# Merging the table, modulation and input-projection stages of a hybrid SSM kernel into one stage

## The reference

```python
mod = cond @ ada_w[i] + ada_b[i]
sh1, sc1, g1, sh2, sc2, g2 = jnp.split(mod, 6, axis=-1)
hn = modulate(rmsnorm(x, norm1_g[i]), sh1, sc1)       # h * (1 + scale) + shift
u = (h @ w_in).astype(f32)                            # input projection, 1024 x 1024
ab_re = mag * jnp.cos(li * dt); ab_im = mag * jnp.sin(li * dt)
# cf = (ab - 1) / lambda; bb = cf * b; then a scan over time with ab, bb, c and d
```

## Time and profile before

| What | Value |
| --- | --- |
| Median of three runs | 6785.2 us |
| Profiled execution | 6783.3 us, span 6781.7 us |
| TensorE busy | 91% of the span |
| VectorE busy | 49% |
| ScalarE busy | 31% |
| GpSimd busy | 26% |
| `ssm_tables` | 2.5 to 82.5 us |
| `ssm_input` | 83.6 to about 523 us |
| `ssm_scan` starts | 523.5 us |

### The profile page before, as it was taken

The page is one execution under the profiler, slowest core; times in us unless marked ns, Lnnn a source line. Parts: engine busy times, 40 slices in busy tenths (PEclk is TensorE's granted clock), DMA queues, the critical chain, the costliest instruction groups (busy, mean ns, idle before and its releaser), DMA issues. The chain is left out here.

```text
span 6781.7 us, 88283 instructions
## 1 busy us (share of the span) xinstructions
PE 6199.4 (91%) x29593; PEld 5085.4 (75%) x29594; DVE 3318.2 (49%) x4653; ACT 2084.9 (31%) x3429; POOL 1734.9 (26%) x1497
## 2 busy tenths in 40 slices
PE   5997888999969999999989999998996899999993
PEld 3875666888847888888868888886774788888883
DVE  5547773443364555565534322223446554556554
ACT  1215553222213433343335200001111333444434
POOL 2763223882022222222210000000001222323222
PEclk8998999999989999999989999998997999999997
DMA  4442335442225766676645534443342565677766
GB/s 140 142 126 89 107 98 174 148 141 99 86 82 187 212 188 193 201 217 200 204 107 206 207 140 158 147 155 125 127 133 99 168 192 166 202 213 243 211 205 242
DMA packets 530877, 1098.31 MB, mean 162 GB/s; under 512 B 49214, under 2 KB 127118, under 8 KB 530778
## 3 DMA queue, kind: packets, MB, share of 16 engines
q1 hardware_dynamic: 418816, 806.11, 34.4%
q0 software_dynamic: 78000, 274.13, 15.8%
q10 hardware_dynamic: 33964, 16.83, 0.8%
HBM read 835.18 MB, written 261.78 MB: 162 GB/s over the span
## 5 line engine op out<-in xcount | busy, mean ns | idle before, releaser
L127 PE MATMUL conv_p<-conv_x_lo,conv_w_hi 128*128 128x512 f32 x1536 | 601.4, 392 | 0.0
L128 PE MATMUL conv_p<-conv_x_hi,conv_w_lo 128*128 128x512 f32 x1536 | 598.7, 390 | 0.0
L129 PE MATMUL conv_p<-conv_x_hi,conv_w_hi 128*128 128x512 f32 x1536 | 598.6, 390 | 0.0
L1835 DVE SCALAR_TENSOR_TENSOR m_o<-m_pO,m_weight_of,m_gate 128x512 f32<-128x512 f32 x320 | 237.6, 747 | 723.9 <-PE m_pO L1555 383.2
L1802 DVE TENSOR_TENSOR m_w_lo<-m_w_raw,m_w_hi 128x1024 fp32r<-128x1024 f32 x496 | 577.9, 1215 | 0.0
L1610 ACT ACTIVATE m_xT_hi<-m_pX 128x512 fp32r<-128x512 f32 x320 | 191.5, 599 | 1151.8 <-PE m_pB L129 993.9
L127 PE MATMUL m_pA<-m_w_lo,m_xT_hi 128*128 128x512 f32 x1280 | 517.2, 404 | 5.7 <-DVE m_xT_lo L1813 5.7
L1551 PE MATMUL m_pO<-m_w_lo,m_hT_hi 128*128 128x512 f32 x1280 | 512.8, 401 | 0.5 <-ACT m_hT_hi L1615 0.5
L1598 ACT ACTIVATE m_w_hi<-m_w_raw 128x1024 fp32r<-128x1024 f32 x512 | 505.3, 1053 | 0.0
L129 PE MATMUL m_pA<-m_w_hi,m_xT_hi 128*128 128x512 f32 x1280 | 502.9, 393 | 0.0
L128 PE MATMUL m_pA<-m_w_hi,m_xT_lo 128*128 128x512 f32 x1280 | 500.1, 391 | 0.0
(11 more groups left out here) (388 smaller groups left out, 12641.4 us busy)
## 6 DMA issues: line engine op xcount, KB each, us to landing
m_w_raw<-in_moe_w_dram SPq DMA_DIRECT2D x384, 1024.0 KB, 7.0
conv_x_hi<-hT_hi SPq DMA_DIRECT2D x24, 2048.0 KB, 8.6
conv_x_lo<-hT_lo SPq DMA_DIRECT2D x24, 2048.0 KB, 13.3
glu_ada<-in_ada_w_dram POOLq DMA_DIRECT2D x96, 256.0 KB, 3.2
a_x<-in_x_dram SPq DMA_DIRECT2D x32, 512.0 KB, 3.6
a_ada<-in_ada_w_dram POOLq DMA_DIRECT2D x64, 256.0 KB, 3.1
u<-a_stage POOLq DMA_DIRECT2D x8, 2048.0 KB, 14.0
s_u<-u SPq DMA_DIRECT2D x64, 256.0 KB, 2.6
```

The source lines that it names most:

```text
L127: pe.matmul(out, lh, rl, start=start, stop=False)
L128: pe.matmul(out, ll, rh, start=False, stop=False)
L129: return pe.matmul(out, lh, rh, start=False, stop=stop)
L1835: dve.scalar_tensor_tensor(out=ob[:, n, :], in0=pO[:, n, :], scalar=wslot[:, bass.ds(tile_, 1)], in1=gate2[:, n, :], op0=ALU.mult, op1=ALU ...
```

## The change

`ssm_tables` and `ssm_input` become one stage, `ssm_front`, and `Modulation` goes.

- The swapped half of b is copied inside SBUF by a DMA on ScalarE's queue, the swapped c is written by VectorE with its sign; TensorE no longer waits for b.
- The modulation product takes the condition broadcast to 128 columns as its weight and adds the bias as a product of a row of ones with the bias row, so the result stands in PSUM on all partitions. The weights are loaded as halves of quarters into buffers that the stage uses later (`stage`, `w_hi`); the quarters of the scale come first.
- The gain is folded straight from PSUM; ScalarE copies the shift out. ScalarE splits the first two pieces of the projection weights before the high part of tile 0.
- The powers move from VectorE to GpSimd. They start when b is done and the fourth quarter is multiplied; GpSimd then clears and starts its partial sums.
- GpSimd stores a finished half first, runs one chunk of partial sums, waits for the store and frees the half. After block 3 a second chunk follows.
- The sums over partitions of the partial sums move into the first two half-iterations of the scan. The partial sums are now the weights (128 columns) and a column of ones is the moving operand, 32 matmuls; the result is transposed and stored as 32 rows of 128.

```diff
+    CHUNKS = (0, 1, 2, 3, 5, 6, 7, 8, 8)
...
-            mod.loads(sp)
+            for n, q in enumerate(ORDER):
+                for h in range(2):
+                    sp.dma_start(ada[q][:, 4 * h:4 * h + 4, :], ada_view[:, 4 * h:4 * h + 4, bass.ts(q, HALF)]).then_inc(m_ld[2 * n + h], 16)
+                if n == 1:
+                    for s in range(2):
+                        sp.dma_start(xb[s][:], x_view[s]).then_inc(x_ld[s], 16)
...
+            for n, q in enumerate(ORDER):
+                out = pU[q // 2][:, q % 2, :]
+                pe.matmul(out, ones[:], bias[0:1, bass.ts(q, HALF)], start=True, stop=False)
+                for k in range(KD):
+                    if k % 4 == 0:
+                        pe.wait_ge(m_ld[2 * n + k // 4], 16)
+                    last = pe.matmul(out, cond[:, 1, k:k + 1].broadcast_to([P, P]), ada[q][:, k, :],
+                                     start=False, stop=k == KD - 1)
+                last.then_inc(m_mm, 1)
...
+            act.wait_ge(x_half, 32)
+            for h in range(2):
+                act.dma_start(Y[h * S:h * S + S], X[S - h * S:P - h * S]).then_inc(y_half, 16)
...
+            std_of(0, 0)
+            act.wait_ge(t_done, 1)
+            act.wait_ge(m_mm, QUARTERS)
+            act.activation(shift[:], shift_ps, ACT.Copy).then_inc(shift_out, 1)
+            split(0)
+            split(1)
+            high(0, 0)
...
+            dve.wait_ge(m_mm, 2)
+            c(stt(out=gain[:], in0=scale_ps, scalar=1.0, in1=gain[:], op0=ALU.add, op1=ALU.mult))
+            normed(c, 0, 0)
...
+            pool.wait_ge(t_done, 1)
+            pool.wait_ge(m_mm, QUARTERS)
+            while m < L:
...
+                c(tt(dr, sr, mr, ALU.mult))
+                c(tt(a, si, mi, ALU.mult))
+                c(tt(di, sr, mi, ALU.mult))
+                c(tt(b, si, mr, ALU.mult))
+                c(tt(dr, dr, a, ALU.subtract))
+                c(tt(di, di, b, ALU.add))
+                m *= 2
...
+            for n in range(NT // BLK):
+                pool.wait_ge(blk_ready, BLK * n + BLK)
+                pool.dma_start(u_view[n ^ 1], stage[:, n % 2, :, :]).then_inc(blk_stored[n % 2], 16)
+                later.run(pool, CHUNKS[n], CHUNKS[n] + (CHUNKS[n + 1] > CHUNKS[n]))
+                pool.wait_ge(blk_stored[n % 2], 16 * (n // 2) + 16)
+                pool.sem_inc(stage_free, 1)
+                later.run(pool, CHUNKS[n] + 1, CHUNKS[n + 1])
```

In `ssm_scan`, on SyncE after the first two u tiles, and on TensorE at the end of the first half-iteration:

```diff
+            sp.dma_start(part[:].rearrange("p (q n) -> p q n", n=HALF), partial[0:SUMS * P // HALF].rearrange("q p n -> p q n")) \
+              .then_inc(sum_ld, 16)
...
+                for n in range(SUMS):
+                    last = pe.matmul(pS[:, n:n + 1], part[:, n * P:(n + 1) * P], ones[:], start=True, stop=True)
+                last.then_inc(sum_psum, 1)
```

More of the change, by code:

```diff
@@ L161, in take @@
         return self.nc.alloc_sbuf_tensor_at(self.tag + name, shape, dt, offset=here)
[L164 to L198, removed]
-                pe.wait_ge(self.out, q - 1)
-            for k in range(KD):
-                last = pe.matmul(self.ps[q % 2][0:1, :], self.cond_sb[:, 1, k:k + 1], self.w[q][:, k, :],
-                                 start=k == 0, stop=k == KD - 1)
-            last.then_inc(self.mm, 1)
-    def results(self, act):
-        for q in range(self.CHUNKS):
-            act.wait_ge(self.mm, q + 1)
-            act.activation(self.row[0:1, bass.ts(q, HALF)], self.ps[q % 2][0:1, :], ACT.Copy).then_inc(self.out, 1)
-    def biases(self, pool):
-        pool.wait_ge(self.b_ld, 16)
-        for q in range(self.CHUNKS):
-            pool.wait_ge(self.out, q + 1)
-            c = bass.ts(q, HALF)
-            pool.tensor_tensor(self.row[0:1, c], self.row[0:1, c], self.bias[0:1, c], ALU.add).then_inc(self.added, 1)
-        pool.wait_ge(self.added, self.CHUNKS)
-        pool.dma_start(self.dst, self.row[:]).then_inc(self.st, 16)
-        pool.wait_ge(self.st, 16)
@@ L319, in ssm_input @@
[L319 to L323 removed]
+        h_hi, h_hi_at = zip(*(core.sb_at(ctx, f"a_hT_hi{s}", [P, KD, P], F32R) for s in range(2)))
+        h_lo, h_lo_at = zip(*(core.sb_at(ctx, f"a_hT_lo{s}", [P, KD, P], F32R) for s in range(2)))
@@ new lines, in ssm_front @@
+        stage, stage_at = core.sb_at(ctx, "a_stage", [P, 2, G, BLK * CH])
+        core.line_up(ctx, "a_ada_first", [P, D])
+        ada_at = -(-nc.sbuf_base // 32) * 32
+        later = PartialSums(core, ctx, "a", cond, ada_w[0][:, 2 * D:], ada_b[0:1, 2 * D:], partial)
+        ones = core.sb(ctx, "a_ones", [1, P])
+        lam, dt_b, sg = core.sb(ctx, "t_lam", [P, 2, S]), core.sb(ctx, "t_dt", [P, G]), core.sb(ctx, "t_sign", [P, 1])
+        small = Region(nc, "t_", shift_at, 4 * D)
+        ab, lt, ki = small.take("ab", [P, 13, G]), small.take("lamT", [P, 2, G]), small.take("turns", [P, G], I32)
@@ L355, in _ @@
-            load_mod(pool, mod_dram, 0, SH1, shift[:], const_ld)
+            c = Chain(pool, sw)
+            pool.sem_inc(stage_free, 2)
             pool.memset(ones[:], 1.0).then_inc(ones_set, 1)
+            c(pool.memset(tab.skip[:], 0.0))
+            pool.dma_start(gain[:], row(norm_g[0:1, :], 0, D)).then_inc(gain_ld, 16)
+            for i in range(4):
+                pool.dma_start(tab.skip[32 * i:32 * i + CH, :], d_skip[0].rearrange("(b i c) -> i c b", i=4, c=CH)[i],
+                               allow_slow_non_contiguous=True).then_inc(skip_ld, 16)
@@ L687, in ssm_scan @@
[L687 removed]
+def ssm_scan(core, ident, tab, u_dram, y_dram, k_dram, partial, mod_dram):
     nc = core.nc
```

424 lines of the change are left out of this document (202 added, 222 removed).

## The result

The changed kernel takes 6745.35 us (median of 5 runs, 6740.56 to 6756.29) beside 6785.2 us (6780.95 to 6787.1) of the kernel before: ratio 0.9944, interval [0.9933, 0.9955]. Forecast: 6748.8 us, range 6732 to 6766, 0.92 for faster by over 13.6 us. The profiled execution has a span of 6743.7 us, 38.0 less than before. So the whole was right. Its parts were not all: two terms were off by 11 and by 5 us, with opposite signs, and a loss of 3 us had been costed at nothing. That these errors nearly cancelled was luck.

What follows compares the result with a forecast made beforehand. TensorE, 91% busy, was taken to bound the kernel, except in three stretches without products. Terms -46.8 + 13.3 - 11.4 + 8.5 = -36.4 us gave a forecast of 6748.8 us, range 6732 to 6766.

Steps and rivals of the forecast that it cites:

- first product: Opening: the input projection's first product comes near 67.2 instead of 113.98 us, -46.8 us (-42 to -49).
- contention, to tile 3's transposes: Early norms: VectorE's w_lo and tile 2's norm wait out GpSimd's powers, +13.3 us (0 to +20).
- stage half for block 6: Steady tiles: the staging half comes free 13.4 us after block 5, TensorE wants it at 23.5; no cost.
- tail: End of the input stage: only the last u store is waited for, -11.4 us (-9.5 to -11.8).
- sums inside the scan: Scan: 64 passes of 7.2 us between two half-iterations plus small extras, +8.5 us (5 to 14).
- Loads, modulation, first product: Opening: last table load near 17.5 us, modulation products about 22.0 to 53.2, first projection product near 67.2.
- Tables beside the products, powers off the path: Opening: VectorE's tables end near 40 us beside the modulation products, costing nothing; the powers' 31.5 us leave the path.
- four w_lo meet 512-element ones, four 1024-element ones: Tile 1's norm: the eight w_lo meet these GpSimd instruction sizes and take 23.8 instead of 12.6 us.
- First u store: Input stage: GpSimd's powers, 70 us with waits, end near 125, before the store is due near 136; no delay.
- the prediction's sign of being wrong: Input stage: a u store coming late by more than 20 us would show the forecast wrong.
- The turn, two copies and a store on ScalarE add a little: Scan: turning, copying and storing the sums add only a little to the 7.2 us of passes.
- sums dearer inside: Rival, chance 0.06: the scan's dependence chain stretches by 20 us instead of 8.5, eating the tail's gain; 6760 us.

Runs made afterwards that it cites:

- The swapped b: Changed kernel with the swapped copy of b loaded from memory through SyncE's queue again, instead of copied inside SBUF: 6748.3 us, ratio 0.9955.
- the run with eight of them: Changed kernel with eight extra 1024-element GpSimd products ahead of the powers, beside w_lo: one execution, 6759.35 us.
- The early release: Changed kernel with GpSimd giving the staging half back midway through the partial-sum chunk after a u store, instead of behind it: 6739.8 us, ratio 0.9937.
- the powers behind tile 2: Changed kernel with GpSimd waiting for the norm of tile 2 before it begins the powers: 6745.2 us, ratio 0.9939.
- the store early: Changed kernel with the sums turned later, but copied and stored ahead of the 2 MB y store instead of right behind it: 6739.2 us, ratio 0.9929.
- the passes in the gaps: Changed kernel with the sums stored ahead of the y store and their 64 one-column passes moved into two TensorE waits: 6736.4 us, ratio 0.9927.
- a scan without sums: Changed kernel with the sums over partitions put back at the end of the input stage, as in the kernel before: 6745.2 us, ratio 0.9938.
- only shortened by the low levels: Changed kernel with powers 2 to 16 on VectorE and the rest on GpSimd behind the norm of tile 2: 6741.1 us, ratio 0.9931.

## Why the prediction was right

In the order of its steps; all in us.

```
term                               forecast   measured   what measured it
first product                       -46.8      -45.5     68.48 against 113.98
contention, to tile 3's transposes  +13.3       +2.4     33.2 against 30.8 behind the first product
stage half for block 6                0         +2.8     356.7 against 353.8 to the last store of u; gap of 2.57
tail                                -11.4      -11.0     51.3 less 40.3
sums inside the scan                 +8.5      +13.8     250.0 against 236.2
sum                                 -36.4      -37.5     722.29 against 759.78 at y 3; span 38.0 less
```

Tile 3's transposes in the kernel before and in the changed one:

```profile
144.81 1.04 PE L423 MATMUL a_pT<-ident,a_hn 128*128 128x128 f32 x8
```

```profile
101.69 1.04 PE L544 MATMUL a_pT<-ident,a_hn 128*128 128x128 f32 x8
```

- **Loads, modulation, first product: right.** Tables landed at 18.8 (17.5 forecast), first modulation product 23.3 (22.0), last one ended 56.0 (53.2), first product 68.5 (67.2). The 1.3 us are the loads; the products were 1.5 us dearer (8.1 a quarter, not 7.8), which a shorter way from the shift to the first product gave back. The swapped b shows that the loads are on this path.
- **Tables beside the products, powers off the path: right.** VectorE was through with b at 38.9 (40 forecast) and idle 13.9 us after the scaling.
- **Contention: mechanism right, term mis-sized.** The forecast had a VectorE instruction with two inputs wait out one running GpSimd tensor_tensor, and so it is. What failed is "four w_lo meet 512-element ones, four 1024-element ones". GpSimd began at 56.2, and was held up by VectorE in its turn, so it was in the 256- and 512-element levels while w_lo ran (66.7 to 81.3): five w_lo met the first, three the second, and none a 1024-element one. The 24 us of the forecast need long instructions, as the run with eight of them showed (20.1). The long ones came when TensorE had 11.8 us of products to cover them. Also, the kernel before paid contention of its own: w_lo took 12.64 there and 9.16 with none; so 2.4 is the difference, and 8.5 the full price (without contention tile 3's transposes stand 24.8 us behind the first product, so the kernel before paid 6.0).
- **What the Trainium skill said of the scaling: the trace agrees in part.** The page SBUF — State Buffer of the Trainium skill (section Who interferes with whom) would have the scaling contend too, with any GpSimd instruction that reads SBUF. Begun while a GpSimd tensor_tensor ran it took 2.33 us (at 95.67), begun while a GpSimd copy ran 2.31 us (at 107.12), against 1.28 alone. The rows of before, never over 1.286 in 32, are no evidence against it for GpSimd's addition (L264): none of the 32 began while it was running. They are evidence against it for GpSimd's scaling (L262), which reads SBUF too: 23 of the 32 began while it had 0.7 to 0.8 us to run, and none was longer for it. In 23 cases the addition (L264) began during VectorE's scaling, and the 23 adds behind (L390) began within it; those are the ones of 2.2 us. In the changed kernel the scaling lost 0.4 us ahead of tile 2's transposes (1.41 in the norm of tile 1 and 1.51 in that of tile 2); the rest fell in the norms of tiles 3 and 4.
- **First u store: right.** 130.5 (136 forecast), powers 56.2 to 127.4 us, 71 us (70 forecast with waits).
- **Steady tiles at no cost: wrong by 2.8.** The forecast compared when the half comes free (13.4 us after block 5) with when TensorE wants the tile behind it (23.5). Both were close: block 5 was ready at 361.6, the half was free at 377.7 (16.1 behind it), TensorE wanted tile 27 at 384.4 (22.8 behind it), 6.7 us of cover. The step that failed left out the chain between them, ScalarE's evacuation and high part, VectorE's low part and norm: 9.2 us from the release to the transposes at 386.99. Block 4's store came 26 us late (24 forecast); the prediction's sign of being wrong, a store of u late by more than 20 us, thus stood against its own forecast. The early release took the gap away, and the powers behind tile 2 showed the same chain at twice the size (6.2).
- **Tail: right.** 13.9 us from the last store's issue to the scan (13.5 forecast).
- **Sums in the scan: too cheap by 5.3.** The passes took 8.57 (7.2), as the clock fell in them. "The turn, two copies and a store on ScalarE add a little" is the step that failed: the store alone held ScalarE 5.26 us and TensorE behind it. With the store early the distance shrinks by 5.3; with the passes in the gaps by 10.0 more. Against a scan without sums they cost 15.2, more than the 13.8 of the table, for the scan itself is 1.4 us shorter than before (234.8 against 236.2), for a reason that stays open. The rival "sums dearer inside" had the place right and the size too high (20).

So the total hit because the contention was priced 11 us too high and the scan and the stage half together 8 too low: the opening and the tail were forecast, that the other errors balance was luck. The range, 6732 to 6766, holds both the result and what each error alone would have made of it.

## What to carry to other kernels

When two engines slow each other, ask which instructions stand beside each other at that moment and how long each is, and look for the stretch in which the bottleneck has work to cover them: the same powers held TensorE for 8.5 us beside w_lo and not at all behind it. Look too at what starting later makes late: all powers behind w_lo gave the 8.5 us back through a late store, and only shortened by the low levels did they keep 6.5. When a buffer's release stands behind other work on its engine, count the whole chain from the release to the engine that starves, not only the two ends. And put small work where the bottleneck already waits, and a small store ahead of a large one on its queue: the sums over partitions cost 15.2 us in one place of the scan and nothing in another.

## What was not expected of the hardware

- A store of 16 KB issued 1.0 us behind a 2 MB store on the same queue held ScalarE for 5.26 us (5.22 to 5.67 in eight runs, 5.46 as eight rows of 2 KB); 8.6 us ahead of the large store it took 0.35.
- In 64 passes with one moving column the granted clock fell from 1.00 to 0.50, and the 64 passes took 8.6 to 9.1 us in seven traces and 11.5 and 11.6 in two others; 16 passes of 512 columns in the same place kept it at 1.00 and took 7.03. Before the passes TensorE had been busy without a gap for 6 us at clock 1.00.
- GpSimd's tensor_tensor on few elements is quicker than its larger forms suggested: from 0.31 us for 64 elements, 0.41 for 128, 0.65 for 256 and 1.10 for 512 where VectorE had nothing long. Beside VectorE even 64 elements took up to 1.45 us; a plain copy of 64 took 1.19 beside it and 0.31 without.
- VectorE and GpSimd seem to take turns: in the run with long products w_lo went from 1.22 to 3.40 us, and GpSimd's products of 1024 elements took 3.20 to 3.46 us against 1.95 free of VectorE, each longer by about the length of the other's.
